# Token lists built once ahead of the expert loop; expert outputs added on VectorE and scattered plainly

## The reference

```
scores = sigmoid(t @ w_router)                    # 576 x 64
top_e  = 8 experts a token, out of 4 of 8 groups
gates  = scores at top_e, normalised, x 2.5
acc   += (silu(t @ wg) * (t @ wu)) @ wd * g[:, None]     # 64 experts, one after the other
shared = (silu(t @ w_gate_s) * (t @ w_up_s)) @ w_down_s
x      = layer_norm(alpha * x + acc + shared)
```

## Time and profile before

| | |
|---|---|
| median of three runs | 1394.04 us (1385.76 to 1397.29) |
| span of the profiled execution | 1394.2 us |
| PE busy | 1241.1 us, 89% |
| DVE busy | 777.2 us, 56% |
| ACT busy | 543.3 us, 39% |
| POOL busy | 407.7 us, 29% |
| moved by DMA | 317.49 MB, mean 228 GB/s |

### The profile page before, as it was taken

One profiled execution on the slowest core, in us unless ns is written; L12 is line 12 of the kernel. 1 busy time (PEld: TensorE's weight loads), 2 busy tenths in 40 slices (PEclk: granted clock), 3 DMA queues, 4 the chain that ended last, 5 costly groups with the idle time before them and its releaser, 6 DMA issues.

```text
span 1394.2 us, 18458 instructions
## 1 busy us (share of the span) xinstructions
PE 1241.1 (89%) x6931; PEld 976.8 (70%) x6931; DVE 777.2 (56%) x1095; ACT 543.3 (39%) x722; POOL 407.7 (29%) x385
## 2 busy tenths in 40 slices
PE   6499978989999899969999999999999999999980
PEld 6499956789999897427666666666666666666650
DVE  2113589243311644537776666666666666666745
ACT  2231467242213312125444444444444444445522
POOL 2000234111100123251433343433444333433223
PEclk9699989599999997989999999999999999999995
DMA  9942020113223308327999999999999999999954
GB/s 191 286 151 81 16 86 2 68 38 100 76 91 115 126 1 343 147 83 276 365 361 350 343 345 343 346 340 342 351 347 342 344 334 341 342 343 342 356 106 152
DMA packets 92096, 317.49 MB, mean 228 GB/s; under 512 B 15586, under 2 KB 48516, under 8 KB 66804
## 3 DMA queue, kind: packets, MB, share of 16 engines
q1 hardware_dynamic: 65616, 257.03, 47.5%
q0 software_dynamic: 19280, 56.12, 20.5%
q10 hardware_dynamic: 7140, 3.50, 0.9%
HBM read 284.30 MB, written 47.97 MB: 238 GB/s over the span
## 4 chain that ended last, share of the span: by engine, by line
PE 77%; DVE 10%; issue 4%; DMA 3%; ACTq 2%; POOL 2%; ACT 2%; DVEq 0%; SPq 0%; POOLq 0%
PE bank L1925 26%; PE bank L1945 16%; PE bank L1661 9%; PE bank L1662 9%; PE bank L1820 4%; DVE onehot L1501 3%; PE bank L1888 3%; PE bank L1676 3%; ACTq L876 2%; PE bank L1850 2%; DVE L L1256 1%; DMA raw<-in_w_in_dram 1%; DVE mx L1262 1%; PE bank L1841 1%; PE bank L1867 1%
## 5 line engine op out<-in xcount | busy, mean ns | idle before, releaser
L1525 DVE TENSOR_TENSOR wgu_lo<-wgu,wgu_hi 128x4096 fp32r<-128x4096 f32 x64 | 282.5, 4414 | 2.7 <-ACT wgu_hi L1125 2.6
L788 POOL TENSOR_TENSOR spare<-spare 128x1 f32<-128x1 f32 x128 | 122.6, 958 | 445.7 <-DMA y_rows<-ysb,idx_u 406.1
L1945 PE MATMUL bank<-wd,hT 128*128 128x512 f32 x512 | 230.1, 592 | 0.9 <-DVE hT L1535 0.9
L1125 ACT ACTIVATE wgu_hi<-wgu 128x4096 fp32r<-128x4096 f32 x63 | 227.4, 3610 | 0.1
L1925 PE MATMUL bank<-wgu_hi,xgT 128*128 128x512 f32 x512 | 206.3, 403 | 2.6
L1925 PE MATMUL bank<-wgu_hi,xgT_lo 128*128 128x512 f32 x512 | 200.9, 392 | 0.0
L1925 PE MATMUL bank<-wgu_lo,xgT 128*128 128x512 f32 x512 | 200.6, 392 | 0.0
L1129 ACT ACTIVATE silu<-bank 128x256 f32<-128x256 f32 x64 | 24.5, 383 | 370.1 <-PE bank L1925 370.1
L1945 PEld LDWEIGHTS bank<-wd,hT 128*128 128x128 f32 x512 | 96.7, 189 | 98.0 <-issue 92.0
L1541 DVE COPY ysb<-bank 128x512 f32<-128x512 f32 x64 | 44.2, 691 | 162.5 <-PE bank L1945 162.5
L1925 PEld LDWEIGHTS bank<-wgu_hi,xgT 128*128 128x128 f32 x512 | 96.7, 189 | 23.4 <-issue 0.5
(11 more groups left out here) (287 smaller groups left out, 2391.6 us busy)
## 6 DMA issues: line engine op xcount, KB each, us to landing
wgu<-in_w_gate_e_dram SPq DMA_DIRECT2D x64, 1024.0 KB, 9.2
wgu<-in_w_up_e_dram SPq DMA_DIRECT2D x64, 1024.0 KB, 13.6
wd<-in_w_down_e_dram SPq DMA_DIRECT2D x64, 1024.0 KB, 7.8
raw<-in_w_in_dram SPq DMA_DIRECT2D x16, 1024.0 KB, 5.5
raw<-in_w_proj_a_dram SPq DMA_DIRECT2D x4, 1024.0 KB, 5.2
raw<-in_w_out_dram SPq DMA_DIRECT2D x4, 1024.0 KB, 5.2
bias_rows<-e_row POOLq DMA_DIRECT2D x1, 3072.0 KB, 34.6
x_lo_kept<-xT_lo SPq DMA_DIRECT2D x1, 2304.0 KB, 10.8
```

What stands on the lines that cost most here:

```text
L788: pool.tensor_tensor(spare[:, i:i + 1], spare[:, 0:1], spare[:, 0:1], ALU.mult).then_inc(s, 1)
L1125: act.activation(wgu_hi[u % 2][:], wgu[u % WSLOTS][:], ACT.Copy).then_inc(hi_by_act, 1)
L1525: v.tensor_tensor(wgu_lo[u % WSLOTS][:], w_[:], wgu_hi[u % 2][:].bitcast(F32), ALU.subtract).then_inc(lo_by_dve, 1)
L1945: last = mm(bank[3 + h][:, :], hT[:, u % 2, j, :], wd[slot][:, j, h * 512:(h + 1) * 512], start=j == 0, stop=j == FE // P - 1)
```

## The change

The token lists are made once. DVE takes each token's eight places from the routing (eight largest of a coded table, slot_u). POOL then scatters token numbers into a table in DRAM, owner, cleared before by SP: 5 tiles x 8 ranks, 40 indirect DMAs of 4 bytes a row. One load brings the lists of all 64 experts into SBUF (idx_all). One-hot, token list, idx and R go; places runs one shared tile earlier. The gates are appended to the rows of x in DRAM (4352 bytes a row instead of 4096), so that a gathered row brings its gates, and the hidden rows are scaled from there.

y is no longer accumulated by the DMA. For each expert POOL gathers its present y rows into yg (gather_y), DVE adds the two output banks to them (y_add), and POOL scatters them back plainly (scatter_y); pads are skipped on both ways. Even and odd experts have an accumulator each, y_rows[0], which starts with alpha x + shared, and y_rows[1], which starts with zeros; at the end both are loaded and added on DVE.

The copy of hT goes from DVE to ACT, the shared expert's product and sum go from POOL and ACT to DVE, the spare operations go, and the expert loop is written out in full.

```diff
+NACC = 2
+FAR_SLOT = 65536
...
     x_lo_kept = nc.dram_tensor("x_lo_kept", (P, DC, TOK), F32, kind="Internal").ap()
-    x1_rows = nc.dram_tensor("x1_rows", (TOK, D), F32, kind="Internal").ap()
-    y_rows = nc.dram_tensor("y_rows", (TOK + P, D), F32, kind="Internal").ap()
+    DG = D + E
+    x1_rows = nc.dram_tensor("x1_rows", (TOK, DG), F32, kind="Internal").ap()
+    y_rows = [nc.dram_tensor(f"y_rows{i}", (TOK, D), F32, kind="Internal").ap() for i in range(NACC)]
...
-                sp.dma_start(x1_rows[a:a + w, :], x1[0:w, t, :]).then_inc(x1_written, 16)
+                sp.dma_start(x1_rows[a:a + w, 0:D], x1[0:w, t, :]).then_inc(x1_written, 16)
...
+            for e in range(2):
+                load_expert(e)
+            sp.wait_ge(gates_dve, 1)
+            for t, (a, w) in enumerate(TILES):
+                sp.dma_start(x1_rows[a:a + w, D:DG], gates[0:w, t, :]).then_inc(gates_written, 16)
+            load_expert(2)
+            rows = owner.rearrange("(t p e) a -> t p (e a)", t=NT, p=P)
+            for t, (a, w) in enumerate(TILES):
+                sp.wait_ge(sy_dve, 2 * (t + 1))
+                sp.dma_start(y_rows[0][a:a + w, :], sy[0:w, t % 2, :]).then_inc(y_inited[t % 2], 16)
...
+            for e in range(3, E):
+                load_expert(e)
...
+            for t, (a, w) in enumerate(TILES):
+                sp.dma_start(x1[0:w, t, :], y_rows[0][a:a + w, :]).then_inc(y_back[t], 16)
+                sp.dma_start(y_other[0:w, t, :], y_rows[1][a:a + w, :]).then_inc(y_back[t], 16)
...
+            pool.wait_ge(owner_cleared, 16 * NT)
+            pool.wait_ge(route_dve, 1)
+            for t, (a, w) in enumerate(TILES):
+                for r in range(8):
+                    pool.indirect_dma_start(out=owner, out_offset=bass.IndirectOffsetOnAxis(slot_u[0:w, t, r:r + 1], 0),
+                                            in_=token_id[0:w, t:t + 1], in_offset=None).then_inc(owner_written, 16)
+
+            pool.wait_ge(owner_written, 16 * NT * 8)
+            pool.dma_start(idx_all[:, :], owner.rearrange("(t p e) a -> t p (e a)", t=NT, p=P)[0]).then_inc(idx_landed, 16)
+
+            def gather_x(slot, at, idx):
+                pool.indirect_dma_start(out=xg[slot][:], out_offset=None, in_=x1_rows,
+                                        in_offset=bass.IndirectOffsetOnAxis(idx, 0),
+                                        bounds_check=bound, oob_is_err=False).then_inc(at, 16)
+
+            def gather_y(i, idx):
+                pool.indirect_dma_start(out=yg[i][:], out_offset=None, in_=y_rows[i],
+                                        in_offset=bass.IndirectOffsetOnAxis(idx, 0),
+                                        bounds_check=bound, oob_is_err=False).then_inc(y_got[i], 16)
+
+            def scatter_y(i, idx):
+                pool.indirect_dma_start(out=y_rows[i], out_offset=bass.IndirectOffsetOnAxis(idx, 0),
+                                        in_=yg[i][:], in_offset=None,
+                                        bounds_check=bound, oob_is_err=False).then_inc(y_put[i], 16)
...
+            pool.wait_ge(gates_written, 16 * NT)
+            pool.wait_ge(rows_cleared, XGSLOTS)
+            pool.wait_ge(idx_landed, 16)
+            for e in range(XGSLOTS):
+                gather_x(e, xg_in[e], idx_all[:, e:e + 1])
             pool.wait_ge(y_inited[0], 16 * ((NT + 1) // 2))
             pool.wait_ge(y_inited[1], 16 * (NT // 2))
-            pool.wait_ge(y_zeroed, 16)
-            for e in range(UNROLL):
-                gather(e + XGSLOTS, (e + XGSLOTS) % UNROLL)
+            gather_y(0, idx_all[:, 0:1])
+            pool.wait_ge(y_zeroed, 16 * NT)
+            gather_y(1, idx_all[:, 1:2])
+            for e in range(E):
                 if e >= 1:
-                    scatter(e - 1, e - 1, e == 1)
-            with pool.Fori(1, E // UNROLL - 1) as i:
-                for u in range(UNROLL):
-                    gather(i * UNROLL + (u + XGSLOTS), (u + XGSLOTS) % UNROLL)
-                    scatter(i * UNROLL + (u - 1), (u - 1) % UNROLL)
-            for e in range(E - UNROLL, E):
+                    pool.wait_ge(y_by_dve, 2 * e)
+                    scatter_y((e - 1) % NACC, idx_all[:, e - 1:e])
+                if e >= NACC:
+                    pool.wait_ge(y_put[e % NACC], 16 * (e // NACC))
+                    gather_y(e % NACC, idx_all[:, e:e + 1])
                 if e + XGSLOTS < E:
-                    gather(e + XGSLOTS, (e + XGSLOTS) % UNROLL)
-                scatter(e - 1, (e - 1) % UNROLL)
-            scatter(E - 1, UNROLL - 1)
-
-            pool.wait_ge(y_added, 16 * E)
+                    pool.wait_ge(h_by_dve, e + 1)
+                    pool.wait_ge(ex_xt, e + 1)
+                    gather_x(e % XGSLOTS, xg_in[e % XGSLOTS], idx_all[:, e + XGSLOTS:e + XGSLOTS + 1])
+            pool.wait_ge(y_by_dve, 2 * E)
+            scatter_y((E - 1) % NACC, idx_all[:, E - 1:E])
+
...
+            def ex_ht_evac(e, u):
+                act.wait_ge(ex_ht, e + 1)
+                act.activation(hT[:, u % 2, :, :], bank[5][:, 0:FE].rearrange("p (j n) -> p j n", j=2),
+                               ACT.Copy).then_inc(ht_by_act, 1)
...
+            for e in range(E):
+                if e + 1 < E:
+                    ex_xt_evac(e + 1, e + 1)
+                if e >= 1:
...
+                    ex_ht_evac(e - 1, e - 1)
                     act.wait_ge(h_by_dve, e)
...
+                ex_silu(e)
+                if e + 2 < E:
+                    weights_hi(e + 2, (e + 2) // WSLOTS + 1)
+            ex_ht_evac(E - 1, E - 1)
...
+            v.wait_ge(pos_done, 1)
+            then(v.scalar_tensor_tensor(slot[:], bank[7][:, 0:NT * E].rearrange("p (t e) -> p t e", t=NT), -float(E),
+                                        slot_base[:].rearrange("p (a e) -> p a e", a=1).to_broadcast([P, NT, E]),
+                                        ALU.mult, ALU.add))
+            then(v.tensor_tensor(slot[:], slot[:], smask[:], ALU.mult))
             for t in range(NT):
-                then(v.memset(R[:, t, :, 1], float(t * P - TOK)))
-
-            v.wait_ge(pos_done, 1)
-            then(v.scalar_tensor_tensor(posm[:], bank[7][:, 0:NT * E].rearrange("p (t e) -> p t e", t=NT), 1.0, smask[:],
-                                        ALU.add, ALU.mult))
-            then(v.tensor_scalar(posm[:], posm[:], -1.0, None, ALU.add))
-            then(v.tensor_scalar(R[:, :, :, 2], posm[:], -1.0, None, ALU.mult))
+                v.max(top8[:, t, :], slot[:, t, :]).then_inc(dve, 1)
+                k[0] += 1
+            v.wait_ge(dve, k[0])
+            v.tensor_scalar(slot_u[:], top8[:], -1.0, float(FAR_SLOT), ALU.mult, ALU.add).then_inc(route_dve, 1)
...
-                v.scalar_tensor_tensor(hh[:, u % 2, :], bank[2][:, FE:2 * FE], gate_idx[:, u % UNROLL, 1:2], silu[:],
+                v.scalar_tensor_tensor(hh[:, u % 2, :], bank[2][:, FE:2 * FE], xg[u % XGSLOTS][:, at], silu[:],
                                        ALU.mult, ALU.mult).then_inc(h_by_dve, 1)
 
-            def ht_evac(e, u):
-                v.wait_ge(ex_ht, e + 1)
-                v.tensor_copy(hT[:, u % 2, :, :], bank[5][:, 0:FE].rearrange("p (j n) -> p j n", j=2)).then_inc(ht_by_dve, 1)
-
-            def y_evac(e, u, free=True):
+            def y_add(e, i):
                 v.wait_ge(ex_dn, e + 1)
-                if free:
-                    v.wait_ge(y_added, (e - 1) * 16)
-                v.tensor_copy(ysb[:, u % 2, 512:1024], bank[4][:, :]).then_inc(y_by_dve, 1)
...
+                for h in range(2):
+                    c = slice(h * 512, (h + 1) * 512)
+                    v.tensor_tensor(yg[i][:, c], yg[i][:, c], bank[3 + h][:, :], ALU.add).then_inc(y_by_dve, 1)
...
+            for e in range(E):
+                if e + 1 < E:
+                    xt_evac(e + 1, e + 1)
+                    weights_lo(e + 1, e + 1)
+                hidden(e, e, slice(D + e, D + e + 1))
+                if e >= 1:
+                    v.wait_ge(y_got[(e - 1) % NACC], 16 * ((e - 1) // NACC + 1))
+                    y_add(e - 1, (e - 1) % NACC)
+            v.wait_ge(y_got[(E - 1) % NACC], 16 * (E // NACC))
+            y_add(E - 1, (E - 1) % NACC)
...
+                if t == 1:
                     places()
-                if t in (NT - 2, NT - 1):
-
-                    pe.wait_ge(route_dve, 1)
-                    for e in range(IDX_AHEAD // 2):
-                        n = e + (t - NT + 2) * (IDX_AHEAD // 2)
-                        token_list(n, n, wait=n > 0)
                 if t >= 1:
                     shared_down(t - 1)
...
-                if wait:
-                    pe.wait_ge(y_by_act, e)
-                    pe.wait_ge(y_by_dve, e)
+                if not (isinstance(e, int) and e == 0):
+                    pe.wait_ge(y_by_dve, 2 * e)
...
+            rows_t(0, 0, 16)
+            for e in range(E):
+                if e + 1 < E:
+                    rows_t(e + 1, e + 1, 16 * ((e + 1) // XGSLOTS + 1))
```

(51 more changed lines are left out.)

359 lines of the change are left out of this document (118 added, 241 removed).

## The result

The changed kernel takes 1609.58 us in the median of four runs (1597.3 to 1617.34), against 1395.03 for the kernel before (four runs too): 1.155 times as long, 95% interval 1.149 to 1.161. The forecast was slower, 1450, with a range to 1600: the direction was right, the size was not, and the time lies outside the range. The profiled execution has a span of 1595.6 us.

What follows compares the result with a forecast made beforehand. The loop was taken as bound by TensorE (10.03 us an expert) plus token lists costing up to 1.6. Profiled 1394.2 + 46 loop + 10 prelude + 3 tail = 1453, rounded to 1450 us; range 1392 to 1600.

Steps and rivals of the forecast that it cites:

- Y: Loop: the start of an expert's y add on DVE, from which the prediction counts its times in us.
- forecast A: Loop: weights_lo holds only the gather of y's issue; 1415 to 1500 us in practice, chance 0.37.
- B: Loop: weights_lo holds the scatter as well; 14.0 to 16.4 us an expert; chance 0.25 including mixtures.
- the gather's landing after its release: Loop: from the end of the held gather of y's issue until its rows land, Y + 7.1 to Y + 10.5 or 12.9.
- The price alone, 3.4: Loop: a lone gather's 4.5 us from issue to landing, less its instruction of 1.07.
- the allowance of up to 2.4: Loop: extra us when 8 gather rows of an engine each wait for one 8 KB weight packet.
- the loop's +46: Loop: 64 experts at a period of 12.1 instead of 11.38 us; bounds +1 and +97.
- The empty queue of the earlier trace: Loop, kernel before: software queue moved no packet from 651.0 to 654.4 after a scatter issued 0.04 before weights_lo; evidence for holding.
- Prelude +10 forecast: Before the loop: 40 table scatters, the list's load and the first gather delay gate_up(0); bounds 0 and +25 us.
- Tail +3 forecast: After the loop: -2 for a quicker last scatter, +5 for extra loads and adds; bounds 0 and +8 us.
- C: Loop: no hold, only the DMA engines bind; 11.4 to 11.7 us an expert, 1408 in all, chance 0.23.
- D: Loop: rows spread better or plain writes cheaper, nothing held, TensorE's 10.03 holds; 1321 us in all, chance 0.15.

Runs made afterwards that it cites:

- e3: Changed kernel with weights_lo subtracting a PSUM column, so one SBUF input instead of two (weights' rest left out of the result): 1435.4 us, ratio 1.033.
- e5: Changed kernel with y returned by accumulating scatter, nothing gathered for y, and the lists' places spread over the partitions in steps of 4: 1329.2 us, ratio 0.954.
- e4: Changed kernel with y returned by the accumulating scatter of the kernel before, no gather of y, places not spread: 1422.3 us, ratio 1.020.
- e6: Changed kernel with only the lists' places spread over the partitions in steps of 4: 1604.7 us, ratio 1.154.
- e8: Changed kernel with weights_lo waiting until the gather of y is issued, gate and up loads split from down's, and places spread: 1402.6 us, ratio 1.003.
- e10: Changed kernel with weights_lo on one SBUF input (weights' rest left out), loads split and places spread: 1412.1 us, no interval.
- e7: Changed kernel with only weights_lo delayed until POOL has issued that round's gather of y, arithmetic unchanged: 1471.7 us, ratio 1.052.
- b1: Kernel before with only its lists' places spread over the partitions in fours: 1394.1 us, ratio 0.9996.

## Why the prediction went wrong

**The mechanism was right.** The add waits for gathered rows; the scatter gets out ahead of weights_lo and the gather of y does not (predicted: issue from Y + 2.5 to 3.0, held until Y + 7.1; measured Y + 2.9 and Y + 7.7). 59 of 64 gathers have an issue of over 4 us; the 0.6 of difference is that the issue ends 0.9 after weights_lo and not with it. That is forecast A, not B: scatters take 1.0. That B's price of 14 stands near the measured 14.25 is chance, since its mechanism does not occur.

**The term that was mis-sized** is the gather's landing after its release: 3.4 to 5.8 us forecast, some 5 taken, 7.8 measured in the median. The price alone, 3.4, was right (3.2 measured), and so was the allowance of up to 2.4 for rows that alternate with weights (the rows took 4.2 instead of 2.5 in the two experts shown). What had no term is the time before the first row: 3.5 after the release instead of 0.7, or some nine weight packets an engine. I had the gather alternate with weights from its first packet on. But the edit also decides when weights are sent: down waits for the add, SP sends 3 MB when down ends, and that falls 0.4 to 2.6 us before the release in most experts. For 3.5 us only weights move, and the alternation follows. So the period is 14.25, not 12.1, and the loop's +46 is +184. I had priced the queue by one landing among weights and not asked what the new wait does to SP's times; e2, which changes only the order of the loads, gives back 67 us.

**The evidence for the hold was misread.** The empty queue of the earlier trace rows was taken as weights_lo holding descriptors of a scatter that had been issued. The missing term explains it as well: SP had sent 3 MB from 647.67 on, 3.3 us before that issue ended. In e3, where weights_lo holds no issue, the queue stays as empty behind a scatter's issue that ends at 793.00 (queues from 793.0 to 796.2; q0 has no row):

```profile
q1 hardware_dynamic: 182, 1.33, 102.3%
```

And in the changed kernel a scatter whose issue ended at 1038.71 moves its rows under a weights_lo that runs from 1038.54 to 1042.95 (1038.7 to 1041.1):

```profile
q0 software_dynamic: 153, 0.26, 27.8%
```

So weights_lo holds an issue that begins under it, as the small operation of the earlier trace rows had suggested, and in these two places not the rows of an issue that is over. That the gather would be held was argued in part from the wrong row, and that much of the hit was luck; rival B loses by the same reading what spoke for it.

**Smaller terms.** Prelude +10 forecast, +8.8 measured: 40 table scatters of 0.91 to 1.10 with gaps of 0.3, two of them longer (3.06 and 4.41). Tail +3 forecast, +9.2 measured, above its bound of 8: the reload of y came 1.5 later behind the last down, not 2 sooner, since the last add waits for its gather, and the five adds lie on DVE's chain, at 1.22 each.

**Rivals.** C, no hold, is refuted by e3: an indirect DMA's issue took 4.84 under a tensor_tensor with two SBUF inputs and 1.03 under one with one. C was drawn from the Trainium skill (SBUF — State Buffer, Who interferes with whom), whose inference is that a tensor_tensor does not stall descriptor writing. The same section's statement that a two-input DVE operation contends with a GpSimd instruction that reads SBUF agrees with these two numbers, as the issue reads its indices in SBUF; whether it is that read which is held, no run here shows. D did not come; e5 shows what it would have needed, no gather of y and rows on all engines, and then comes near its time (1329 against 1321). That the loaded half of the engines matters was right, but in e4, not here (e6).

**Still open.** Why a gather behind weights moves no row until some nine weight packets an engine are through, and then needs 6 to 8 to land even with the loads split and the rows spread (e8, e10), was not taken apart further. The parts of a round are read from one execution of each kernel.

## What to carry to other kernels

A DMA that is only sent may be slow; one whose result an engine waits for must be counted from the wait to the landing, with everything that the new wait itself delays or sends off at the same time. Ask of each issue on POOL which long DVE operation with two SBUF inputs it will meet, and let that operation wait if the path needs the issue (e7). When a compute term is taken out of a loop whose DMA engines are nearly full, see first on which engines the rows lie: the same spreading was worth nothing in two kernels (e6, b1) and 93 us in the third (e5).

## What was not expected of the hardware

A gather whose issue ended about 1 us after 3 MB of weights had been asked for on another queue moved its first packet 3.5 us later and landed after 7.8; one whose issue ended 0.3 before them, on idle DMA engines, landed after 3.2. A difference of some 1.4 us in the order of requests costs 4.6 at the landing.

The granted clock fell where PE waited. In this window of the changed kernel it is 0.50, the lower of the two levels, after PE had stood waiting for the add:

```profile
1055.00:1056.40 1.40, 1.40 (x3) 0.66 (x2) 1.40 (x1) 0.00 (x0) 1.40 (x1) 0.50 0.46 179
```

Over the loop it was 0.89 to 0.93. The eight matmuls of down took 3.67 at a granted clock of 1.00, 5.14 at a mean of 0.71 and 6.60 at 0.55 (three experts of the changed kernel):

```profile
933.63 3.67 PE L1857 MATMUL bank<-wd,hT 128*128 128x512 f32 x8 [2.71 <-DVE yg L1493]
```

```profile
1022.08 5.14 PE L1857 MATMUL bank<-wd,hT 128*128 128x512 f32 x8 [3.19 <-DVE yg L1493]
```

```profile
1053.26 6.60 PE L1857 MATMUL bank<-wd,hT 128*128 128x512 f32 x8 [3.00 <-DVE yg L1493]
```

The add waits for the gather and not for PE, and yet the clock reaches the path: SP's loads leave when down ends, here 5.1, 6.6 and 8.1 after the add, and the release is at 7.7. So it is the slowest down that lets the gather go ahead of the weights, and the next add begins 15.1, 15.5 and 11.0 after this one. In all 12 experts with a quick landing down took 6.3 or more, and in the other 44 at most 5.4. No run changes the clock alone, so this is read from the order of times.
